# A hybrid decoder step on one core: the rows of act_hi and act_lo kept 272 elements apart instead of 264

## The reference, cut to what matters

```python
h = _rms_norm(x, norm_g)
z = h @ w_in                                   # 2048 -> 14*512 + 8 + 4*2048 columns
...
ys = jnp.stack([y_ret, y_gdn, y_sc, y_pool], axis=2)
proj = jnp.einsum('btnc,ncd->btnd', ys, w_branch)
gates = jax.nn.sigmoid(merge_logits.reshape(Bn, T, N_BRANCH, D_MODEL))
merged = jnp.sum(gates * proj, axis=2)
out = x + merged @ w_out
```

## Time and profile before

| | before |
|---|---|
| median of 3 runs | 2051.76 us (2049.7 to 2053.64) |
| span of the profiled execution, first to last instruction | 2049.6 us |
| TensorE matmul busy | 1992.3 us, 97%, 16294 instructions |
| VectorE busy | 1346.1 us, 66% |
| ScalarE busy | 1113.6 us, 54% |
| GpSimd busy | 186.5 us, 9% |
| mean granted TensorE clock | 0.993 |

### The profile page before, as it was taken

How to read it: one execution, slowest core, us unless ns; L and a number is a source line. 1 busy time by engine, 2 the same in 40 slices (tenths; PEclk the granted TensorE clock), 3 DMA queues, 4 the chain that set the end, 5 groups by cost and what they waited for, 6 DMA issues and landing times.

```text
span 2049.6 us, 50596 instructions
## 1 busy us (share of the span) xinstructions
PE 1992.3 (97%) x16294; PEld 1976.0 (96%) x16294; DVE 1346.1 (66%) x2608; ACT 1113.6 (54%) x2045; POOL 186.5 (9%) x345
## 2 busy tenths in 40 slices
PE   6999999999999999999999999999999999999996
PEld 6999999999999999999999999999999999999996
DVE  7887566755656556666678766676565656566666
ACT  5556556645455555555555655655464645455554
POOL 2111110110101010000011210001010100100000
PEclk9999999999999999999999999999999999999998
DMA  6655555555554545665656555655555555566664
GB/s 209 190 175 172 157 181 162 184 160 156 154 172 135 176 140 167 188 180 180 184 172 184 171 173 155 190 164 175 165 162 160 162 155 149 160 175 179 178 184 161
DMA packets 183252, 348.13 MB, mean 170 GB/s; under 512 B 20592, under 2 KB 20720, under 8 KB 182992
## 3 DMA queue, kind: packets, MB, share of 16 engines
q1 hardware_dynamic: 177552, 326.45, 53.4%
q0 software_dynamic: 5568, 19.80, 3.0%
HBM read 333.61 MB, written 12.56 MB: 169 GB/s over the span
## 4 chain that ended last, share of the span: by engine, by line
PE 90%; DVE 4%; issue 3%; ACT 2%; DMA 1%; DVEq 0%; ACTq 0%; SPq 0%
PE acc L1301 27%; PE acc L1302 27%; PE acc L1303 26%; DMA raw<-w_stream 1%; PE side L1514 1%; PE side L1488 1%; DVE wlo L829 1%; PE side L1512 1%; PE side L1505 1%; ACT whi L540 1%; PE side L1396 1%; PE side L1495 1%; PE side L1402 1%; PE side L1358 1%; DVE act_lo L841 0%
## 5 line engine op out<-in xcount | busy, mean ns | idle before, releaser
L829 DVE TENSOR_TENSOR wlo<-raw,whi 128x512 fp32r<-128x512 f32 x1219 | 828.3, 694 | 488.4 <-ACT whi L540 481.4
L540 ACT ACTIVATE whi<-raw 128x512 fp32r<-128x512 f32 x1219 | 751.5, 628 | 643.7 <-PE acc L1303 553.9
L1301 PE MATMUL acc<-act_hi,whi 128*128 128x264 f32 x3328 | 972.6, 292 | 40.1 <-issue 19.6
L1303 PE MATMUL acc<-act_hi,wlo 128*128 128x264 f32 x3328 | 947.8, 285 | 0.0
L1302 PE MATMUL acc<-act_lo,whi 128*128 128x264 f32 x3328 | 947.2, 285 | 0.0
L1301 PEld LDWEIGHTS acc<-act_hi,whi 128*128 128x128 f32 x3328 | 631.8, 190 | 48.2 <-issue 35.9
L1302 PEld LDWEIGHTS acc<-act_lo,whi 128*128 128x128 f32 x3328 | 632.8, 190 | 0.9
L1303 PEld LDWEIGHTS acc<-act_hi,wlo 128*128 128x128 f32 x3328 | 629.4, 189 | 0.0
L1301 PE MATMUL acc<-y_hi,whi 128*128 128x264 f32 x1536 | 439.9, 286 | 0.0
L1302 PE MATMUL acc<-y_lo,whi 128*128 128x264 f32 x1536 | 435.4, 283 | 0.0
L1303 PE MATMUL acc<-y_hi,wlo 128*128 128x264 f32 x1536 | 434.8, 283 | 0.0
(11 more groups left out here) (267 smaller groups left out, 1438.2 us busy)
## 6 DMA issues: line engine op xcount, KB each, us to landing
raw<-w_stream SPq DMA_DIRECT2D x1220, 256.0 KB, 2.8
state<-ret_in POOLq DMA_DIRECT2D x8, 512.0 KB, 5.5
s_ret<-state POOLq DMA_DIRECT2D x8, 512.0 KB, 4.6
state<-gdn_in POOLq DMA_DIRECT2D x8, 512.0 KB, 5.4
s_gdn<-state POOLq DMA_DIRECT2D x8, 512.0 KB, 6.1
x<-x_in SPq DMA_DIRECT2D x4, 528.0 KB, 6.5
y_out<-wide SPq DMA_DIRECT2D x4, 396.0 KB, 2.8
con<-consts SPq DMA_DIRECT2D x1, 1582.0 KB, 11.8
```

The source lines that it names most:

```text
L540: sc.activation(whi[:, s, :], raw[:, s, :], ACT.Copy).then_inc(hi_ready, 1)
L829: ve.tensor_tensor(wlo[:, s, :], raw[:, s, :], whi[:, s, :].bitcast(F32), ALU.subtract).then_inc(lo_ready, 1)
L1301: mm(acc[bank][:, 0:N], w_h, hi[:, k0 + k, :], start=first and k == 0, stop=False)
L1303: op = mm(acc[bank][:, 0:N], w_l, hi[:, k0 + k, :], start=False, stop=last and k == UK - 1)
```

## The change

The two arrays are allocated with rows of 272 elements, and all uses see the first 264 of each.

```diff
+NPAD = -(-N // 16) * 16
...
-        act_hi = sb("act_hi", [KT, N], F32R)
-        act_lo = sb("act_lo", [KT, N], F32R)
+        act_hi = sb("act_hi", [KT, NPAD], F32R)[:, :, 0:N]
+        act_lo = sb("act_lo", [KT, NPAD], F32R)[:, :, 0:N]
```

## The result

| | before | after |
|---|---|---|
| median | 2051.61 us (2047.45 to 2054.24, 20 runs) | 2055.25 us (2052.3 to 2059.91, 20 runs) |
| ratio to before | | 1.0020, 95% interval 1.0014 to 1.0026 |
| span of the profiled execution | 2049.6 us | 2055.3 us |

A forecast was written before the change was run, and what follows sets the result against it. TensorE, 97% busy, was taken as the bound, through the distance between big matmul starts. Only the matmuls on act rows counted, -6.2 us, all else 0: 2051.8 - 6.2 = 2045.6 us, range 2035 to 2061.

The forecast's parts named there:

- What bounds the kernel: Whole kernel: TensorE busy 97%, time nearly the number of big matmuls times the distance between their starts, 0.121 us.
- the address matters: Big matmul units: the starting row's place between multiples of 256 bytes sets 1.44 or 1.46 us, about 1%.
- The weights' width is thus not what costs: Matmuls at L1358 with weights of only 8 columns also take 0.121 us each, so width does not set the distance.
- the big matmuls on act rows: 832 act units, all beginning where k0 = 0 began, were to save 0.0075 us each: 6.2 us less.
- The rival of no change: Big matmuls: places shift starts to and fro but a stream's mean stays; time 2051.8 us, chance 26%.
- The slower rival: Act units: rows at 64, 128 and 192 bytes meet a bad phase, 1.46 us; 8.3 us more, 2060.1, chance 22%.
- The excess goes: Big matmuls with all rows at multiples of 64 bytes run at 0.111 us: 100 us less, 1952, chance 6%.
- Terms at nothing: Matmuls on y rows, added register instructions and copies of four rows were each counted as 0.
- The y units of R and O: Big matmuls on y rows in these stages: rows still 1056 bytes apart, expected 1.44 and 1.46 us as before.
- The register instructions: Extra ones on VectorE, ScalarE and GpSimd: at most 3.8 us on VectorE, under its idle time, counted 0.
- The copies of four rows: Copies on ScalarE and GpSimd, 1.07 us each, might take twice as long; done 18 us before needed, counted 0.

The follow-up runs named there:

- e2_shift128: Kernel of before, rows still 1056 bytes apart, act_hi and act_lo moved 128 bytes on, y_hi and y_lo 256; ratio 0.9998.
- e1_streams: Kernel of before plus 18 unused matmul streams at its end, varied in row distance, offset and columns; per 12 matmuls, rows 1056 apart 1.458 and 1.442 us.
- e13_groups: Kernel of before with 128 unused bytes behind every fourth row in all four arrays, two helpers sharing memory; every unit 1.453 us, ratio 0.9999.
- e14_groups_act: Kernel of before with 128 unused bytes behind every fourth row of act_hi and act_lo alone; ratio 1.0000.
- e8_hi_only: Kernel of before with rows 1088 bytes apart in act_hi alone, act_lo keeping 1056; ratio 1.0031.
- e15_groups_act128: Kernel of before with 128 unused bytes behind every fourth act row and both act arrays 128 bytes further on; act units 1.463 us, ratio 1.0038.
- e9_addresses: Kernel of before, rows 1056 bytes apart, 512 unused bytes ahead of act_lo and of y_hi, so arrays begin where the change has them; ratio 1.0007.
- e3_y_only: Kernel of before with rows 1088 bytes apart in y_hi and y_lo alone, act rows staying 1056 apart; ratio 1.0024.
- e4_both: Kernel of before with rows 1088 bytes apart in all four arrays, two 32-byte helpers sharing memory with other tensors; ratio 1.0026.
- e5_streams2: Kernel of before plus 22 unused matmul streams at its end, varying columns, row distance, low-row shift and entry; one row throughout at 264 columns took 288 cycles.
- e11_streams3: The change plus 18 unused streams at its end; rows 1088 apart took 1.450 and 1.457 us behind odd-place matmuls, 1.473 behind float32 sums.
- e12_again: The change executed once more, unaltered; mean distance between big matmuls 121.35 ns again.
- e16_streams4: The change plus 8 unused streams at its end repeating the row order of whole stages; stage X gave 1.459, 1.465, 1.473, 1.473 and 1.456 us.
- e6_265: Kernel of before with act rows of 265 elements, 1060 bytes apart; act units 1.469 to 1.490 us, ratio 1.0082.

## Why the prediction was wrong, step by step

**What bounds the kernel** held. The total followed the distance between big matmuls. So did "the address matters": e2_shift128 turned the pattern round by 128 bytes. "The weights' width is thus not what costs" held for most of the excess, not all: 8 columns took 0.007 us off a unit's mean in e1_streams.

**The step that failed** is the one on the big matmuls on act rows, "The nearest are the units that begin there now: 1.44 us", and with it the -6.2 us. It had two faults. It priced a unit by its starting place, though a unit's time is not its own: e13_groups gave all units exactly the places of the 1.442 units and measured 1.453. In before such a unit stands between two of 1.458, and only the sum of the pair, 2.900, is a price. And it took rows at 0, 64, 128 and 192 bytes for rows at 0, 32, 64 and 96. They run at 1.450 and 1.457 in one rhythm, 0.003 above the mean of before, and at 1.473 in another, 0.023 above. The forecast's term was -0.0075 a unit on 832 units; the mean of undisturbed act matmuls went from 121.01 to 121.52 ns, which is +0.006 a unit, +5 us.

**The rival of no change** had the right remark, that what went before counts and that a gain may be given back by the next unit. It is what e13_groups and e14_groups_act found for that edit. For the change it fell short by the stages in the rhythm of 1.473. Its argument that no row touches more blocks says nothing about the size of the effect: e8_hi_only and e15_groups_act128 touch no more either. The rule on lines of 16 bytes that it took from the Trainium skill (SBUF — State Buffer, Specifications) fits in that rows off a multiple of 16 bytes are the dearest, 1.520 in e1_streams, but is no full account, since rows at multiples of 16 differ by up to 2% (1.440 and 1.467).

**The slower rival** was right in sign. Its size, 8.3 us, was twice too large, but the mean act unit, 1.458, is above the 1.455 from which it was to decide. That rows at 64, 128 and 192 bytes cost more than those of before is what happened. Whether it is a phase with the weights' loads or with the previous row, as it had offered, is not shown: the weights' slot plays no part in e1_streams, but weights of 8 columns ended the pattern of the rows 1056 apart. The 2055.25 us lie within the range of 2035 to 2061, by the bound taken from the slowest unit and not by the forecast's reasoning.

**The excess goes** is refuted: rows of 264 columns all at multiples of 64 bytes never took less than 1.440 us in any stream or stage here, and most took more.

**Terms at nothing** came out near nothing, one of them for a reason that the prediction had wrong. The y units of R and O kept their times. Those of X did not, 1.465 before and 1.456 after, and the prediction had named a change of y units as a fault in its reasons: it is the same fault, a unit's time taken as its own. Over all y matmuls the mean went from 120.94 to 120.99 ns, 0.2 us in all. The register instructions appear in after as 24 of 40 ns on VectorE and 8 of 35 ns on ScalarE, 1.2 us under idle time. At the edge of the two layers, from the eighth-last unit of O to the thirteenth of G, the change took 34.7 us against 33.3, but e9_addresses, with the rows of before and none of these instructions, took 34.6, so this is not their price. The copies of four rows took what they had the earlier trace rows, 1.07 us on ScalarE and 1.06 on GpSimd:

```profile
L812 DVEq ALU_OP  x24: 40/40/40, 950.0 to 2041.0; - x24
L516 ACTq ALU_OP  x8: 35/35/35, 943.3 to 2022.7; - x8
L592 ACT ACTIVATE act_hi<-y_hi x8: 1070/1072/1072, 123.3 to 1205.3; - x8
L406 POOL CAST act_lo<-y_lo x8: 1062/1062/1538, 122.0 to 1202.1; - x8
```

**What stays open.** Which circuit makes the rhythms was not looked for: the runs show that the moving rows' addresses and their sequence carry them, not why rows 1088 apart have several, nor what part the weights' loads have. Nor is it shown what picks 1.473 at the start of e3_y_only's stage R, from its second unit on, three units ahead of the first float32 sum of that stage. Rows 2048 bytes apart ran at 1.440 in a stream, 0.7% below the mean of before; four arrays of 16 such rows would take 63488 bytes more in a partition, where e4_both had to share two helpers to find room for 2048, and it was not tried.

## What to carry to other kernels

A difference between neighbouring instructions in a stream is not a price for either of them: add up a whole period before you move one. Making rows begin at rounder addresses is no gain by itself; here rows 1056 bytes apart, in the places of before or 128 bytes on, had a lower mean than rows 1060, 1072 or 1088 apart. Where an engine is 97% busy with one kind of instruction, compare its mean distance between starts, to a tenth of a per cent, from one profiled execution: it put twelve kernels in nearly the order of their total times, which alone could hardly tell most of them apart.

## What the runs showed of the hardware that was not expected

- A float32r matmul of 128x128 weights, in a stream over one row at the array's start, takes 24 to 38 cycles of 2.4 GHz more than its columns, from 248 to 512 of them (276 cycles for 248, 288 for 264, 544 for 512; e5_streams2, e11_streams3). At 128 columns, rows 1088 bytes apart, it takes 268 cycles, 0.112 us (e1_streams), near the 0.105 us a pass that one column took the earlier trace rows.
- One row used throughout takes 288 cycles at 0, 16, 64 and 128 bytes, 293 at 32 bytes and 304 at 4 bytes (e1_streams).
- The same instructions at the same addresses ran at 1.450 and 1.457 or at 1.473 us per 12, by what preceded them (e11_streams3). A second execution repeated the unit times of the stages X, R and O, but not which units of G took 1.450 and which 1.457 (e12_again).
- A sequence of rows carries its unit times from a stage full of other engines' work to a stream with all other engines idle unchanged, 1.459, 1.465, 1.473, 1.473 and 1.456 (e16_streams4, the stream behind four float32 sums).
- A unit's time can change with its rows untouched: the y units of X took 1.465 before, 1.456 in the change and 1.434 with act rows 1060 bytes apart (e6_265).
